# Latent queries of the sample rows, computed in the last head pair of the prompt part instead of at the start of the sample part

## The chip, the cores and the metric

The kernel runs on one core of one Trainium2 chip. The metric is device time of one execution in microseconds (us), and the times are medians of several executions. The trace comes from one profiled execution.

## The reference

One inference step of a decoder trunk with two layers, in float32, for 1024 prompt rows and 8 × 4 = 32 sample rows. Layer 0 has sliding-window attention, layer 1 multi-head latent attention; each is followed by a mixture of 64 experts. The change lies in layer 1. For the sample rows, cut to what matters:

```
q_lat  = einsum('bthd,chd->bthc', qn, w_uk)
s_past = (einsum('bthc,bsc->bhts', q_lat, past_c) + einsum('bthr,bsr->bhts', qr, past_r)) * scale
s_new  = (einsum('bthc,bsc->bhts', q_lat, c) + einsum('bthr,bsr->bhts', qr, kr)) * scale
p      = softmax(concatenate([s_past, s_new]))
o_lat  = p @ [past_c, c];  o = einsum('bthc,chd->bthd', o_lat, w_uv);  y = o @ w_o
```

There are 16 heads of 64 (nope) + 32 (rope) columns, a latent of 256 columns, 8 batch rows with 4 new positions each and 1024 past positions in 8 pages of 128. The prompt rows take the ordinary way: keys `c @ w_uk` and values `c @ w_uv` for each head, causal attention over 1024 positions.

## The kernel before

The kernel is a row of phases. Each phase is a block in which the five engines run their own instruction lists and wait for semaphores; it ends with all engines meeting. Layer 1's attention has three of them: `mla_projection_phase`, `mla_prompt_phase` (tiles with the prefix `h_`) and `mla_sample_phase` (prefix `g_`).

**The prompt part** loops over 8 head pairs `cc` and in each over 16 units `u` (a query block `n` of 128 rows and one head `s` of the pair); `m = 16 * cc + u`. TensorE does, in this order for each m: `scores(m + 2)` (L2340), `turn(m)`, which transposes the probabilities (L2360), in units 8 and 9 the product of the next pair's keys (`keys`, L2317), and a piece of the values product (L2382). VectorE adds the causal mask and takes the maximum (L2285, L2286), ScalarE the exponential (L2201); both copy transposed probabilities out of PSUM. Scores lie in `ps_s[:, m % 2]`, two banks each; keys go to the second bank of one half, `ps_s[:, half, 512:]`, which is free from unit 8 (or 9) until unit 12 (or 13), since the units between are narrow. `keys_out` on ScalarE (even head) and VectorE (odd head) copies them to `kT` right after the step u − 1 = 8 or 9, and `scores` of unit 12 or 13 waits for that. In the last pair there is no next pair: units 8 and 9 have no key product, and the two banks stand empty. SP loads in this phase, among others, the sample rows' queries (`ahead["qn"]`, `ahead["qr"]`), the first pages of the cache, and, after the last keys, w_uk a second time in a turned layout (`uk_in`, L2173).

**The sample part** works on pairs of batch rows, i = 0 to 3. TensorE first waits for `uk_in` and computes the latent queries (L2629): for 8 head pairs, 2 halves `k` of the latent and 2 heads `s`, a product of 64 × 128 weights with 32 columns, into the first two banks of `ps_p`, one bank for each `s`. Each call is two instructions in the trace. Then ScalarE (s = 1) and VectorE (s = 0) copy them to `qlat` (`query_part`, L2503, L2525). TensorE waits for these copies (`ql_done`) and for `qr_done`, that is for `qrb`, in which VectorE lays out the rotary queries (a memset L2518 and four copies L2520). Then come `scores(0, 0)`, `scores(0, 1)` (latent part L2574, rotary part L2580), `new_scores` (L2593), `scores(1, 0)`, `turn(0)` (L2599), `scores(1, 1)`, `values(0)` (L2611) and so on. SP and POOL issue the pages (L2464, 272 KB each): from the start of the phase those of batch rows 2 (second half) to 5, and those of rows 6 and 7 when `values(0)` and `values(1)` are done (`o_made`), on SP with the output weights `w_o` behind them. `scores(i, 0)` waits for all pages of batch rows 2i and 2i + 1.

The functions:

Of the kernel before, what the change touches and what calls it, by code (L numbers as in the profile page):

```python
# [21 lines left out]
P = 128  # L22
D = 1024
SEQ = 1024
NB = 8
NT = 4
NS = NB * NT
# [4 lines left out]
HEADS = 16  # L32
# [8 lines left out]
NOPE = 64  # L41
ROPE = 32
# [2034 lines left out]
def mla_prompt_phase(nc, io, dram, cst, cT, krT, oT_all, w_uv, wk, v, ahead, qT_out, q_stored, places, over_v, pages_in, uk_in):  # L2077
# [38 lines left out]
    with ExitStack() as stack:  # L2116
# [16 lines left out]
        ps_o = c.ps("ps_o", [P, 2, 512])  # L2133
        rot_in, ahead_in = c.sem("rot_in"), c.sem("ahead_in")
        q_in = c.sems("q_in", 2)
        q_done = c.sem("q_done")
# [4 lines left out]
        o_made, o_done = c.sems("o_made", 2), c.sems("o_done", 2)  # L2141
        block = stack.enter_context(nc.Block())

        @block.sync
# [38 lines left out]
        def _(eng):  # L2183
# [39 lines left out]
            for m in range(NU * PAIRS):  # L2223
                cc, u = m // NU, m % NU
                exps(m)
                if m:
                    probs_out(m - 1)
                if u - 1 in KEYS_AT and cc + 1 < PAIRS:
                    keys_out(cc + 1, KEYS_AT.index(u - 1))
                if u == RD_AT[1] + 1:  # L2230
                    recips_out(2 * cc)
                if u == RD_AT[0] + 1 and cc:
                    recips_out(2 * cc - 1)
# [4 lines left out]
        def _(eng):  # L2238
# [41 lines left out]
            for m in range(NU * PAIRS):  # L2280
                cc, u = m // NU, m % NU
                g, n, s = UNITS[u]
                width = P * (n + 1)
                eng.wait_ge(s_made, m + 1)
                ch.link(eng.tensor_tensor(ps_s[:, m % 2, P * n:width], ps_s[:, m % 2, P * n:width], cst["causal"][:], ALU.add))  # L2285
                eng.tensor_reduce(nm[:, u:u + 1], ps_s[:, m % 2, 0:width], AX.X, ALU.max, negate=True).then_inc(nm_done, 1)  # L2286
                if m:
                    probs_out(m - 1)
                if u - 1 in KEYS_AT and cc + 1 < PAIRS:
                    keys_out(cc + 1, KEYS_AT.index(u - 1))  # L2290
                if u % 8 == 3 and m > 3:
                    recips(m // 8 - 1)
                if u in Q_AT and cc + 1 < PAIRS:
                    queries_turned(cc + 1, Q_AT.index(u) // 2, 1 - Q_AT.index(u) % 2)
                if u == NU - 1:
                    rows_out(2 * cc)
                if u == 7 and cc:
                    rows_out(2 * cc - 1)
# [5 lines left out]
        def _(eng):  # L2304
# [9 lines left out]
            def keys(cc, half):  # L2314
# [4 lines left out]
                ins.then_inc(kn_made, 1)  # L2319

            def scores(m):
                cc, u = m // NU, m % NU
# [8 lines left out]
                if u - 4 in KEYS_AT and cc + 1 < PAIRS:  # L2331
                    for sem in (kn_even, kn_odd):
                        eng.wait_ge(sem, 2 * cc + KEYS_AT.index(u - 4) + 3)
                if u == (RD_AT[0] + 4) and cc:
                    eng.wait_ge(rd_done, 2 * cc)
# [57 lines left out]
            for m in range(NU * PAIRS):  # L2393
                cc, u = m // NU, m % NU
                r = m // 8 - 1
                if m + 2 < NU * PAIRS:
                    scores(m + 2)
                turn(m)
                if u in KEYS_AT and cc + 1 < PAIRS:
                    keys(cc + 1, KEYS_AT.index(u))  # L2400
                if u == RD_AT[1]:
                    recips_turn(2 * cc)
                if u == RD_AT[0] and cc:
                    recips_turn(2 * cc - 1)
                if r >= 0 and u % 8 < 6:
                    values(r, u % 8)
# [5 lines left out]
def mla_sample_phase(nc, io, dram, cst, cT, krT, c_sample, oT_all, w_uv, w_ukT, ahead, places, over_v, pages_in, uk_in, w_o):  # L2412
# [7 lines left out]
    with ExitStack() as stack:  # L2420
# [3 lines left out]
        qrb = c.sb("qrb", [P, NB, P // ROPE, R])  # L2424
        qlat = c.sb("qlat", [P, 2, NB, HEADS, NT])
        p = c.sb("p", [P, SEQ + NS])
# [5 lines left out]
        ol = c.sb("ol", [P, KVL])  # L2432
        uk = w_ukT[:].rearrange("p c n -> p (c n)").rearrange("p (h k j) -> p h k j", h=HEADS // 2, k=2)
        olT = w_ukT[:].rearrange("p c n -> p (c n)")[:, 0:2 * HEADS * NS].rearrange("p (k h b t) -> p k h b t", k=2, h=HEADS, b=NB)
# [10 lines left out]
        def half_pages(b, half):  # L2445

            if b == 2 and half:
# [4 lines left out]

        (new_made, qr_done, ql_made, ql_done, s_made, sn_done, p_done, pT_made, pA_done, pD_done, o_made, o_done, oT_made, oT_done, y_made, y_done, chain,
         den_done) = (c.sem(n) for n in (
             "new_made", "qr_done", "ql_made", "ql_done", "s_made", "sn_done", "p_done", "pT_made", "pA_done", "pD_done", "o_made", "o_done", "oT_made",
             "oT_done", "y_made", "y_done", "chain", "den_done"))
# [36 lines left out]

        def query_part(k, s):

            src = ps_p[:, 512 * s + 256 * k:512 * s + 256 * k + 256].rearrange("p (c b t) -> p c b t", c=HEADS // 2, b=NB)
            return qlat[:, k].rearrange("p b (c s) t -> p s c b t", s=2)[:, s], src

        @block.scalar
        def _(eng):  # L2500
            eng.wait_ge(ql_made, 1)
            for s in range(2):
                eng.copy(*query_part(s, 1)).then_inc(ql_done, 1)  # L2503
            for i in range(BP):
# [11 lines left out]
        def _(eng):  # L2516
# [5 lines left out]
            ch.link(eng.memset(oT_all[:, :, SEQ + NS:], 0.0))  # L2522
            eng.wait_ge(ql_made, 1)
            for s in range(2):
                eng.tensor_copy(*query_part(s, 0)).then_inc(ql_done, 1)  # L2525

            eng.wait_ge(new_made, 1)
# [31 lines left out]
        def _(eng):  # L2559
            flat = lambda ap: ap.rearrange("p h t -> p (h t)")  # L2560

            def scores(i, half):
# [8 lines left out]
                for k in range(2):  # L2571
                    for j in range(2):
                        b = 2 * i + j
                        eng.matmul(ps_s[R * j:R * j + R, i % 2, cols], flat(qlat[:, k, b]), half_pages(b, half)[:, :, P * k:P * k + P],  # L2574
                                   start=k == 0, stop=False)
                for r in range(P // ROPE):
                    for j in range(2):
# [44 lines left out]

            eng.wait_ge(uk_in, 16)
            for cc in range(HEADS // 2):
                for k in range(2):
                    for s in range(2):
                        r = slice(NOPE * s, NOPE * s + NOPE)
                        at = 512 * s + 256 * k + NS * cc
                        ins = eng.matmul(ps_p[:, at:at + NS], uk[r, cc, k, :], qn[r, cc, :], start=True, stop=True)  # L2629
            ins.then_inc(ql_made, 1)  # L2630
            eng.wait_ge(qr_done, P // ROPE)
            eng.wait_ge(ql_done, 4)
            scores(0, 0)
# [207 lines left out]
def build(nc, io):  # L2841
# [10 lines left out]
    with ExitStack() as stack:  # L2852
# [10 lines left out]
        for layer in range(2):  # L2863
            with ExitStack() as outer:
# [4 lines left out]
                else:  # L2869
                    with ExitStack() as lat:  # L2870
                        a = lambda n, sh: lat.enter_context(nc.sbuf_tensor(n, sh, F32))
                        cT, krT, c_sample = a("cT", [P, 2, ROWS]), a("krT", [QD, ROWS]), a("c_sample", [NS, KVL])
                        w_uv, w_uk = a("w_uv", [P, 2, HEADS * HD]), a("w_uk", [P, 2, HEADS * NOPE])
                        ahead = {"qn": a("qn", [P, HEADS // 2, NS]), "qr": a("qr", [QD, HEADS, NS]), "mask": a("mask", [P, NB // 2, NS])}
                        ahead["table"] = lat.enter_context(nc.sbuf_tensor("table", [1, NB * PAGES], I32))
# [56 lines left out]
```

## Time and profile before

| | us |
|---|---|
| median of 3 executions | 2445.76 |
| lowest, highest | 2437.91, 2449.31 |
| the profiled execution, its own time | 2443.78 |
| its span in the trace | 2442.1 |
| TensorE matmul busy | 2136.4 |
| VectorE, ScalarE, GpSimd busy | 834.7, 625.5, 222.1 |
| TensorE's mean granted clock (1 is full) | 0.948 |

Times inside the trace are counted from the start of the span. The prompt part of the second attention ends near 1624, and the sample part runs from there to 1699. A timeline row gives start, length, engine, line, operation, tiles and, in brackets, how long the engine was idle before and what ended that. Rows of equal instructions are merged ("x32"). A matmul's length includes its way through the array, so that the pace of a row of them is read from one start to the next.

### The profile page before, as it was taken

The page shows a single profiled execution, that of the slowest core. Times are in us where ns is not written, and L with a number is a line of the kernel's source. Part 1 is how long each engine was busy: PE and PEld are TensorE (multiplying, and loading weights), DVE is VectorE, ACT ScalarE, POOL GpSimd, SP SyncE. Part 2 cuts the span into 40 slices and gives each one's busy share as a digit, 9 for nine tenths or more (in the row PEclk, how much of TensorE's full clock was granted, in tenths as well). Part 3 has the DMA queues.
Part 4 walks back from the last instruction along what each step waited for, and adds up shares of the span by engine and source line. Part 5 has one row for each costly group of instructions (what it writes and reads, how often), then busy time and mean ns, then how long its engine had stood idle before and what let it go on. Part 6 is the DMA issues. An engine that isn't in the chain of part 4 may idle for free. (4 is left out here: it accounts for less than half of the span.)

```text
span 2442.1 us, 27707 instructions
## 1 busy us (share of the span) xinstructions
PE 2136.4 (87%) x9976; PEld 1045.8 (43%) x9976; DVE 834.7 (34%) x2196; ACT 625.5 (26%) x1399; POOL 222.1 (9%) x330
## 2 busy tenths in 40 slices
PE   6999989998887877879998999997998888788886
PEld 3444445563333333345544555554555333333333
DVE  1544445651221111123416666642553221111114
ACT  2444442111111111123425555531111111111114
POOL 0010101101111111100000000010000111101103
PEclk9999988999999999989999999998998999989998
DMA  6000007339999999975550010345527999999997
GB/s 230 18 9 18 5 1 274 120 135 398 419 418 419 419 418 415 408 295 169 135 94 14 14 27 14 100 146 179 207 93 295 418 418 418 419 417 416 416 387 301
DMA packets 175980, 580.97 MB, mean 238 GB/s; under 512 B 80066, under 2 KB 83746, under 8 KB 124914
## 3 DMA queue, kind: packets, MB, share of 16 engines
q1 hardware_dynamic: 90354, 501.76, 51.8%
q10 hardware_dynamic: 64160, 35.42, 4.9%
q0 software_dynamic: 21328, 41.99, 4.6%
q8 instruction: 83, 1.36, 0.2%
q14 instruction: 55, 0.45, 0.1%
HBM read 541.39 MB, written 73.37 MB: 252 GB/s over the span
## 5 line engine op out<-in xcount | busy, mean ns | idle before, releaser
L1586 PE MATMUL m_ps_gu<-ring,m_xT 128*64 128x512 f32 x2080 | 509.9, 647 | 102.3 <-issue 99.0
L1586 PEld LDWEIGHTS m_ps_gu<-ring,m_xT 128*64 128x64 f32 x2080 | 173.2, 148 | 433.3 <-issue 427.8
L1595 PE MATMUL m_ps_y<-ring,m_hT 128*64 128x512 f32 x1040 | 250.7, 626 | 68.5 <-DVE m_hT L1441 68.0
L1485 PE MATMUL m_ps_y<-w_o,oT_all 128*128 128x512 f32 x512 | 231.4, 601 | 3.6 <-PEq L174 3.6
L1435 DVE TENSOR_TENSOR m_h<-m_act,m_ps_gu 128x256 f32<-128x256 f32 x64 | 26.9, 421 | 591.7 <-ACT m_act L1172 591.7
L584 PE MATMUL a_ps_q<-a_w,a_hT 128*128 128x512 f32 x384 | 181.5, 614 | 4.8 <-DMA a_w<-swa_w_qkv 3.5
L2340 PE MATMUL h_ps_s<-h_kT,h_qT 96*128 96x512 f32 (+3 forms) x384 | 158.6, 523 | 14.3 <-ACT h_p L2201 12.2
L1172 ACT ACTIVATE m_act<-m_ps_gu 128x256 f32<-128x256 f32 x64 | 24.5, 383 | 557.0 <-PE m_ps_gu L1586 557.0
L1595 PEld LDWEIGHTS m_ps_y<-ring,m_hT 128*64 128x64 f32 x1040 | 72.3, 142 | 202.1 <-issue 121.2
L1089 POOL DMA_INDIRECT expert_rows<-m_y,m_rows_i x64 | 64.5, 1007 | 869.6 <-DVE m_y L1445 844.7
L1485 PEld LDWEIGHTS m_ps_y<-w_o,oT_all 128*128 128x128 f32 x512 | 95.0, 193 | 107.2 <-issue 107.2
L1445 DVE COPY m_y<-m_ps_y 128x512 f32<-128x512 f32 x64 | 44.3, 692 | 258.5 <-PE m_ps_y L1595 258.5
L2201 ACT ACTIVATE h_p<-h_ps_s,h_nm 128x128 f32<-128x128 f32 (+7 forms) x128 | 94.8, 741 | 106.8 <-DVE h_nm L2286 106.0
L1143 ACT COPY m_y<-m_ps_y 128x512 f32<-128x512 f32 x64 | 37.4, 585 | 280.4 <-PE m_ps_y L1595 280.4
L584 PEld LDWEIGHTS a_ps_q<-a_w,a_hT 128*128 128x128 f32 x384 | 70.2, 194 | 89.2 <-issue 86.9
L2340 PEld LDWEIGHTS h_ps_s<-h_kT,h_qT 96*128 96x128 f32 x384 | 63.1, 190 | 94.7 <-issue 68.9
L2286 DVE TENSOR_REDUCE h_nm<-h_ps_s 128x1 f32<-128x128 f32 (+7 forms) x128 | 97.0, 758 | 4.4
L374 ACT ACTIVATE a_p<-a_s,a_nm 128x256 f32<-128x256 f32 x128 | 64.0, 501 | 115.0 <-DVEq L510 114.2
L1050 POOL DMA_INDIRECT m_xg<-normed,m_toks_i x64 | 65.3, 1020 | 272.1 <-DVEq L1296 242.1
L1571 PEld LDWEIGHTS m_ps_x<-ident,m_xg 128*128 128x128 f32 x512 | 63.3, 195 | 58.7 <-issue 58.7
L2360 PE MATMUL h_ps_p<-ident,h_p 128*128 128x128 f32 x576 | 84.4, 273 | 0.8 <-ACT h_p L2201 0.7
L1571 PE MATMUL m_ps_x<-ident,m_xg 128*128 128x128 f32 x512 | 75.8, 292 | 8.0 <-DMA m_xg<-normed,m_toks_i 8.0
(418 smaller groups left out, 2587.8 us busy)
## 6 DMA issues: line engine op xcount, KB each, us to landing
ring<-moe_w_down SPq DMA_DIRECT2D x130, 1024.0 KB, 23.7
ring<-moe_w_gate SPq DMA_DIRECT2D x124, 1024.0 KB, 21.6
ring<-moe_w_up SPq DMA_DIRECT2D x124, 1024.0 KB, 23.9
ring<-expert_rows SPq DMA_DIRECT2D x16, 1024.0 KB, 8.9
x_ffn<-misc ACTq DMA_DIRECT2D x18, 512.0 KB, 5.4
normed<-m_y ACTq DMA_DIRECT2D x18, 512.0 KB, 3.6
places<-mla_pages SPq DMA_DIRECT2D x30, 272.0 KB, 3.3
a_w<-swa_w_qkv SPq DMA_DIRECT2D x12, 512.0 KB, 11.0
```

The source lines that it names most:

```text
L374: eng.activation(p[:, m % 2, j, :], s[:, m % 2, j, :], ACT.Exp, bias=nm[:, hh:hh + 1], accum_out=den[:, hh:hh + 1]).then_inc(p_done, 1)
L584: ins = eng.matmul(ps_q[:], hT[:, t % 2, k, :], w[:, k, 512 * n:512 * n + 512], start=k == 0, stop=k == KC - 1)
L1050: eng.indirect_dma_start(out=xg[:, k % 3, :], out_offset=None, in_=dram["normed"], in_offset=bass.IndirectOffsetOnAxis(ap=toks_i[:, k:k + ...
L1089: eng.indirect_dma_start(out=dram["expert_rows"], out_offset=bass.IndirectOffsetOnAxis(ap=rows_i[:, k:k + 1], axis=0), in_=y[:, k % 2, :], ...
L1485: ins = eng.matmul(ps_y[:, n, :], oT_all[:, k, P * t:P * t + P], w_o[:, k, 512 * n:512 * n + 512], start=k == 0, stop=k == KC - 1)
L1571: ins = eng.transpose(ps_x[:, P * i:P * i + P], xg[:, k % 3, i::KC], ident[:])
L1586: ins = eng.matmul(gu_now[r], xT_now[:, i, r], w[:, slot, s, 0:2, DE * i:DE * i + DE], start=i == 0, stop=i == KC - 1)
L1595: ins = eng.matmul(ps_y[r, n, :], hT[:, i, r], w[:, slot, s, 2, D * i + 512 * n:D * i + 512 * n + 512], start=i == 0, stop=i == 1)
L2201: eng.activation(p[:, m % 2, 0:width], ps_s[:, m % 2, 0:width], ACT.Exp, bias=nm[:, m % NU:m % NU + 1], accum_out=den[:, g, PLACE[n], s:s ...
L2286: eng.tensor_reduce(nm[:, u:u + 1], ps_s[:, m % 2, 0:width], AX.X, ALU.max, negate=True).then_inc(nm_done, 1)
L2340: ins = eng.matmul(ps_s[:, m % 2, a:b], qT[cc % 2][:, s, P * n:P * n + P], kT[cc % 2][:, s, a:b], start=True, stop=True)
L2360: ins = eng.transpose(ps_p[:, at + P * t:at + P * t + P], p[:, m % 2, P * t:P * t + P], ident[:])
```

## The change

- `query_latents(s)` does the same 32 calls in `mla_prompt_phase`, in the last head pair, those of s = 0 in the step of unit 8 and those of s = 1 in the step of unit 9, after `turn` and before the values product. They write to the second bank of `ps_s[:, s]`, where the other pairs have their keys. All calls of one step have the same `s`.
- ScalarE copies the result for s = 0 and VectorE that for s = 1, at the places where `keys_out` stands in the other pairs. `scores` of units 12 and 13 wait for these copies.
- `qlat` becomes a buffer of the outer scope (4 KB of each partition), so that it outlives the prompt part.
- In the sample part the products, the copies and their wait are gone. The wait for `qr_done` moves from before `scores(0, 0)` to before its rotary part.

```diff
+            def query_latents(s):
+                if s == 0:
+                    eng.wait_ge(ahead_in, 16 * 6)
+                    eng.wait_ge(uk_in, 16)
+                r = slice(NOPE * s, NOPE * s + NOPE)
+                for h in range(PAIRS):
+                    for k in range(2):
+                        at = 512 + 256 * k + NS * h
+                        ins = eng.matmul(ps_s[:, s, at:at + NS], uk[r, h, k, :], ahead["qn"][r, h, :], start=True, stop=True)
+                ins.then_inc(ql_made, 1)
...
# TensorE, scores(m) of the prompt part
+                if u - 4 in KEYS_AT and cc + 1 == PAIRS:
+                    eng.wait_ge((ql_even, ql_odd)[KEYS_AT.index(u - 4)], 2)
...
-                if u in KEYS_AT and cc + 1 < PAIRS:
-                    keys(cc + 1, KEYS_AT.index(u))
+                if u in KEYS_AT:
+                    if cc + 1 < PAIRS:
+                        keys(cc + 1, KEYS_AT.index(u))
+                    else:
+                        query_latents(KEYS_AT.index(u))
...
# ScalarE; VectorE the same with KEYS_AT[1], ql_made 2, tensor_copy, query_part(k, 1) and ql_odd
+                if u - 1 == KEYS_AT[0] and cc + 1 == PAIRS:
+                    eng.wait_ge(ql_made, 1)
+                    for k in range(2):
+                        eng.copy(*query_part(k, 0)).then_inc(ql_even, 1)
...
# the sample part
-            eng.wait_ge(uk_in, 16)
-            for cc in range(HEADS // 2):
-                for k in range(2):
-                    for s in range(2):
-                        r = slice(NOPE * s, NOPE * s + NOPE)
-                        at = 512 * s + 256 * k + NS * cc
-                        ins = eng.matmul(ps_p[:, at:at + NS], uk[r, cc, k, :], qn[r, cc, :], start=True, stop=True)
-            ins.then_inc(ql_made, 1)
-            eng.wait_ge(qr_done, P // ROPE)
-            eng.wait_ge(ql_done, 4)
             scores(0, 0)
...
+                if i == 0 and half == 0:
+                    eng.wait_ge(qr_done, P // ROPE)
                 for r in range(P // ROPE):
```

## Rows read from the trace of the kernel before

**Rows 1.** The page's first line.

```profile
span 2442.1 us, 27707 instructions
```

**Rows 2.** Timeline of TensorE, last pair but one, unit 8.

```profile
1562.00 1.88 PE L2317 MATMUL h_ps_s<-cT,w_uk 128*128 128x512 f32 x4
1563.81 1.08 PE L2382 MATMUL h_ps_o<-h_pT,v_rows 128*64 128x256 f32 x8
```

**Rows 3.** Timeline of TensorE, last pair, unit 8.

```profile
1602.61 0.82 PE L2360 MATMUL h_ps_p<-ident,h_p 128*128 128x128 f32 x6
1603.36 1.08 PE L2382 MATMUL h_ps_o<-h_pT,v_rows 128*64 128x256 f32 x8
```

**Rows 4.** Timeline of VectorE: maxima of units 8 and 15, in the last two pairs.

```profile
1558.56 0.96 DVE L2286 TENSOR_REDUCE h_nm<-h_ps_s 128x1 f32<-128x768 f32 x1
...
1579.12 0.69 DVE L2286 TENSOR_REDUCE h_nm<-h_ps_s 128x1 f32<-128x512 f32 x1
...
1599.82 0.96 DVE L2286 TENSOR_REDUCE h_nm<-h_ps_s 128x1 f32<-128x768 f32 x1
...
1616.35 0.69 DVE L2286 TENSOR_REDUCE h_nm<-h_ps_s 128x1 f32<-128x512 f32 x1
```

**Rows 5.** TensorE's waits, 1581 to 1624: us in total, times, longest.

```profile
PE h_ps_s L2340 <- ACT h_p L2201: 0.9, 2, 0.6
PE h_ps_p L2360 <- ACT h_p L2201: 0.7, 1, 0.7
```

**Rows 6.** Timeline of the engines, start of the sample part.

```profile
1624.96 5.20 PE L2629 MATMUL g_ps_p<-qn,w_uk 64*128 64x32 f32 x64 [1.62 <-PEq L174]
...
1627.22 1.80 DVE L2520 COPY g_qrb<-qr 32x512 f32<-32x512 f32 x4
...
1631.13 1.09 PE L2574 MATMUL g_ps_s<-over_v,g_qlat 128*64 128x512 f32 x1 [0.97 <-issue]
...
1634.22 0.27 PE L2580 MATMUL g_ps_s<-over_v,g_qrb 128*64 128x128 f32 x1
...
1639.99 0.64 PE L2574 MATMUL g_ps_s<-over_v,g_qlat 128*64 128x512 f32 x1
...
1640.11 0.29 DVE L2528 TENSOR_TENSOR g_sn<-g_ps_n,mask 128x128 f32<-128x128 f32 x1 [9.08 <-PE g_ps_n L2593]
...
1643.88 1.09 PE L2599 MATMUL g_ps_p<-ident,g_p 128*128 128x128 f32 x8 [1.08 <-ACT g_p L2510]
```

**Rows 7.** Engines in stretches of 1 us: busy, TensorE's clock, DMA share, GB/s.

```profile
1627.00:1628.00 1.00, 1.00 (x15) 1.00 (x14) 0.93 (x3) 0.00 (x0) 0.81 (x2) 0.51 0.71 126
...
1633.00:1634.00 1.00, 1.00 (x6) 0.35 (x4) 0.00 (x0) 0.00 (x0) 0.00 (x0) 0.57 1.12 350
```

**Rows 8.** Page loads issued from 1631.3 to 1631.9.

```profile
L2464 SPq DMA_DIRECT2D places<-mla_pages x1: 333/333/333, 1631.5 to 1631.5; - x1
...
DMA to landing us min/median/max: 6.3/6.7/7.3
```

**Rows 9.** The same view as rows 7, when the first page loads end.

```profile
1649.00:1650.00 1.00, 1.00 (x12) 0.67 (x10) 0.31 (x2) 0.56 (x1) 0.00 (x0) 1.00 0.29 111
```

**Rows 10.** TensorE's waits after 1640: us in total, times, longest.

```profile
PE g_ps_s L2574 <- DMA places<-mla_pages: 12.3, 1, 12.3
```

**Rows 11.** L2629 alone: TensorE busy, weight loads busy, clock, DMA share, GB/s.

```profile
1624.96:1627.00 2.04, 2.04 (x37) 2.04 (x38) 1.00 0.01 4
```

**Rows 12.** Timeline of TensorE in the expert phase: small matmuls and what follows.

```profile
1732.69 1.90 PE L1510 MATMUL m_ps_gu<-m_wr,m_xT 128*128 128x72 f32 x16
1734.43 5.36 PE L1485 MATMUL m_ps_y<-w_o,oT_all 128*128 128x512 f32 x12
1739.63 0.53 PE L1528 MATMUL m_ps_h<-m_cols,m_slots 128*128 128x32 f32 x4
1739.99 0.41 PE L1517 MATMUL m_ps_gu<-m_ohs,before 128*128 128x64 f32 x2
```

**Rows 13.** SP's load of w_uk in the turned layout.

```profile
L2173 SPq DMA_DIRECT2D w_uk<-mla_w_uk_turned x1: 339/339/339, 1568.1 to 1568.1; - x1
```

More of the change, by code:

```diff
@@ L2134, in mla_prompt_phase @@
         rot_in, ahead_in = c.sem("rot_in"), c.sem("ahead_in")
+        ql_made, ql_even, ql_odd = c.sem("ql_made"), c.sem("ql_even"), c.sem("ql_odd")
+        uk = wk[:].rearrange("p c n -> p (c n)").rearrange("p (h k j) -> p h k j", h=PAIRS, k=2)
         q_in = c.sems("q_in", 2)
@@ L2142, in mla_prompt_phase, with query_part @@
         block = stack.enter_context(nc.Block())
+        def query_part(k, s):
+            src = ps_s[:, s, 512 + 256 * k:512 + 256 * k + 256].rearrange("p (c b t) -> p c b t", c=PAIRS, b=NB)
+            return ahead["qlat"][:, k].rearrange("p b (c s) t -> p s c b t", s=2)[:, s], src
         @block.sync
@@ L2290, in _ @@
                     keys_out(cc + 1, KEYS_AT.index(u - 1))
+                if u - 1 == KEYS_AT[1] and cc + 1 == PAIRS:
+                    eng.wait_ge(ql_made, 2)
+                    for k in range(2):
+                        eng.tensor_copy(*query_part(k, 1)).then_inc(ql_odd, 1)
                 if u % 8 == 3 and m > 3:
@@ L2319, in keys @@
                 ins.then_inc(kn_made, 1)
+            def query_latents(s):
[4 more added lines that the diff above has]
+                for h in range(PAIRS):
+                    for k in range(2):
+                        at = 512 + 256 * k + NS * h
+                        ins = eng.matmul(ps_s[:, s, at:at + NS], uk[r, h, k, :], ahead["qn"][r, h, :], start=True, stop=True)
+                ins.then_inc(ql_made, 1)
             def scores(m):
@@ L2424, in mla_sample_phase @@
         qrb = c.sb("qrb", [P, NB, P // ROPE, R])
-        qlat = c.sb("qlat", [P, 2, NB, HEADS, NT])
+        qlat = ahead["qlat"]
         p = c.sb("p", [P, SEQ + NS])
@@ L2432, in mla_sample_phase @@
         ol = c.sb("ol", [P, KVL])
-        uk = w_ukT[:].rearrange("p c n -> p (c n)").rearrange("p (h k j) -> p h k j", h=HEADS // 2, k=2)
         olT = w_ukT[:].rearrange("p c n -> p (c n)")[:, 0:2 * HEADS * NS].rearrange("p (k h b t) -> p k h b t", k=2, h=HEADS, b=NB)
@@ L2451, in half_pages @@
             return tensor[:, at:at + H]
-        (new_made, qr_done, ql_made, ql_done, s_made, sn_done, p_done, pT_made, pA_done, pD_done, o_made, o_done, oT_made, oT_done, y_made, y_done, chain,
+        (new_made, qr_done, s_made, sn_done, p_done, pT_made, pA_done, pD_done, o_made, o_done, oT_made, oT_done, y_made, y_done, chain,
          den_done) = (c.sem(n) for n in (
-             "new_made", "qr_done", "ql_made", "ql_done", "s_made", "sn_done", "p_done", "pT_made", "pA_done", "pD_done", "o_made", "o_done", "oT_made",
+             "new_made", "qr_done", "s_made", "sn_done", "p_done", "pT_made", "pA_done", "pD_done", "o_made", "o_done", "oT_made",
              "oT_done", "y_made", "y_done", "chain", "den_done"))
@@ L2492, in _ @@
             load_pages(eng, odd, 1, 7)
-        def query_part(k, s):
-            src = ps_p[:, 512 * s + 256 * k:512 * s + 256 * k + 256].rearrange("p (c b t) -> p c b t", c=HEADS // 2, b=NB)
-            return qlat[:, k].rearrange("p b (c s) t -> p s c b t", s=2)[:, s], src
         @block.scalar
         def _(eng):
-            eng.wait_ge(ql_made, 1)
-            for s in range(2):
-                eng.copy(*query_part(s, 1)).then_inc(ql_done, 1)
             for i in range(BP):
@@ L2522, in _ @@
             ch.link(eng.memset(oT_all[:, :, SEQ + NS:], 0.0))
-            eng.wait_ge(ql_made, 1)
-            for s in range(2):
-                eng.tensor_copy(*query_part(s, 0)).then_inc(ql_done, 1)
             eng.wait_ge(new_made, 1)
@@ L2621, in rows_turn @@
                 ins.then_inc(oT_made, 1)
-            eng.wait_ge(uk_in, 16)
-            for cc in range(HEADS // 2):
-                for k in range(2):
-                    for s in range(2):
-                        r = slice(NOPE * s, NOPE * s + NOPE)
-                        at = 512 * s + 256 * k + NS * cc
-                        ins = eng.matmul(ps_p[:, at:at + NS], uk[r, cc, k, :], qn[r, cc, :], start=True, stop=True)
-            ins.then_inc(ql_made, 1)
-            eng.wait_ge(qr_done, P // ROPE)
-            eng.wait_ge(ql_done, 4)
             scores(0, 0)
@@ L2873, in build @@
                         w_uv, w_uk = a("w_uv", [P, 2, HEADS * HD]), a("w_uk", [P, 2, HEADS * NOPE])
-                        ahead = {"qn": a("qn", [P, HEADS // 2, NS]), "qr": a("qr", [QD, HEADS, NS]), "mask": a("mask", [P, NB // 2, NS])}
+                        ahead = {"qn": a("qn", [P, HEADS // 2, NS]), "qr": a("qr", [QD, HEADS, NS]), "mask": a("mask", [P, NB // 2, NS]),
+                                 "qlat": a("qlat", [P, 2, NB, HEADS, NT])}
                         ahead["table"] = lat.enter_context(nc.sbuf_tensor("table", [1, NB * PAGES], I32))
```

## The prediction

> **What bounds the kernel now.** I read the page first. Its chain of what ended last reaches back only through the final phase, so it doesn't speak of this place; the page gives the span, 2442.1 us [rows 1]. The change touches two stretches, the last head pair of the prompt part and the first 20 us of the sample part. So I read the timelines of TensorE, VectorE and ScalarE over both.
>
> In the prompt part TensorE sets the pace. In the pair before the last, the key product of unit 8 starts at 1562.00 and the next thing starts at 1563.81 [rows 2]: a slot of 1.81 us with nothing idle behind it. In the last pair the transposes at 1602.61 run straight into the values product at 1603.36 [rows 3]. That the keys' slots are fully exposed can be read from VectorE's maxima: from unit 8 to unit 15 it takes 1579.12 − 1558.56 = 20.56 us with keys and 1616.35 − 1599.82 = 16.53 us without [rows 4]. The difference, 4.03 us, is two slots (3.62 us) and 0.4 more. From 1581 on TensorE waits 1.6 us in all in the last pair [rows 5].
>
> In the sample part the order is different. TensorE begins at 1624.96 with the latent queries, starts the first scores of pages at 1631.13, their rotary part at 1634.22, the second batch pair's scores at 1639.99, and turns the first probabilities at 1643.88, after a wait of 1.08 us for ScalarE; VectorE had started on the new rows' scores at 1640.11 [rows 6]. The granted clock of TensorE is at the lower level (0.5, 1.2 GHz) from 1627.0 on and comes back to 2.4 GHz late in the stretch that starts at 1633 [rows 7].
>
> **What is taken out of the sample part.** The 32 calls (64 instructions) of the latent queries, four copies, and the wait for them. TensorE can start the page scores at once, at 1624.96 if the start of the phase is held still. After some 1.7 us it meets the new wait: the rotary part needs qrb, whose four copies start at 1627.22 and take 1.80 us [rows 6], so until 1629.0. Behind this wait in TensorE's queue are the rest of scores(0, ·) and new_scores. From the rotary part (1634.22) to the end of new_scores (1639.99) it took 5.8 us, nearly all at the full clock. So new_scores would end near 1629.1 + 5.8 = 1634.9, or about 1637.4 if the lower clock holds for 5 of these us (half of 5 is lost): 2.6 to 5.1 us earlier than before.
>
> What is late next is a transfer. scores(1, 0) waits for the pages of batch rows 2 and 3. SP and POOL issue them from the start of the phase on, at times that the change doesn't touch. The last of these on SP goes out at 1631.5, and the three issued between 1631.3 and 1631.9 take 6.3 to 7.3 us to land [rows 8]: the last is there near 1631.5 + 7.3 = 1638.8. In the kernel before that was hidden, as TensorE came at 1639.99, only 1.2 us later. In the changed kernel TensorE comes early and waits until 1638.8. Then 1642.80 − 1639.99 = 2.81 us of scores (the end is 1643.88 less the idle 1.08 [rows 6]) end at 1641.6, and turn(0) follows at once: its exponentials are through 3.9 us after new_scores (1643.88 less 1639.99), which is 1638.8 to 1641.3. So turn(0) starts at 1641.6 instead of 1643.88, and the gain is **2.3 us**, not the 6.2 us between 1624.96 and 1631.13 that the removed work took. From below: were the landing no gate, turn(0) would come at 1638.8 to 1641.3, a gain of 5.1 to 2.6. From above: a clock that falls in the new waits takes 1.5 us or more of it back.
>
> Does the rest follow? values(0) and o_made come 2.3 us earlier. That releases the next pages, and the output weights behind them on SP. The first batches of pages keep the DMA engines busy only until about 1649.3, as the share of 0.29 in the stretch from 1649 shows [rows 9]; so the next loads can start earlier. The 12.3 us that TensorE later waits for pages [rows 10] is the tail of that transfer, and it moves with its start. Everything behind (projection, experts, final norm) begins at the end of this phase. I let the 2.3 us through whole.
>
> **What is put into the last pair.** The same 64 instructions, in two slots of 32, after turn(8) and turn(9), where TensorE is the bound [rows 2 to 5]. Their price is what has to be chosen. Before, s alternated from call to call: s = 0 reads partitions 0 to 63 and s = 1 reads 64 to 127. 37 of them fell into 2.04 us at the full clock, 0.055 us each [rows 11]. In the new loops all calls of a slot have the same s, so neighbours use the same half of the array. The nearest rows of matmuls that can't share the array are the slot sums' (L1528, 128 loaded columns, 32 moving): 4 of them take 1739.99 − 1739.63 = 0.36 us, 0.09 each; and the router's (L1510, 128 loaded, 72 moving): 16 take 1734.43 − 1732.69 = 1.74 us, 0.109 each [rows 12]. I take 0.09, as both sizes match: 64 × 0.09 = **5.8 us**. The bounds are 64 × 0.055 = 3.5 and 64 × 0.109 = 7.0.
>
> The Trainium skill (TensorE: Matmul & The Clock Gate, Part 3, The mechanism) says that a weight load overlaps matmuls in flight only when it goes to another row group. That speaks against the grouping by s, and it is on the side of the 5.8. If loads overlapped whatever the group, as the page's queue with its background buffer might let one hope, the slots would cost 3.5.
>
> The copies: ScalarE gets two of 256 columns behind slot 0 and VectorE two behind slot 1. Behind the wait for ql_made on ScalarE stands exps(10), behind the one on VectorE the maximum of unit 11. In the pair before, keys_out stands at these places; scores(13) needs the exponentials of unit 11, and TensorE gets to scores(13) 3.6 us after its slot (a values product, scores(12), turn(10) and values again), while 0.8 us of copies, 0.9 us of maxima and 0.8 us of exponentials make 2.5. I cost them at nothing; if the cover were gone it would be the 0.8 us of VectorE's copies. The two other new waits on TensorE are long over: w_uk's second content is issued at 1568.1 [rows 13], 35 us before the slot. The 4 KB that qlat now takes in the outer buffers moves addresses only.
>
> **Sum.** +5.8 in the prompt part, −2.3 in the sample part: +3.5 us. The profiled execution is 2443.8 us by its own time (span 2442.1 and 1.7 around it), so 2447.3. It lies 2.0 below the median shown, 2445.8, so a median of **2449 us**, 0.14% above before. The three times shown spread over 11 us; 0.5% (12 us) is about what a measurement of this kernel can tell from no change, so this is no change by that measure.
>
> **The rivals.**
>
> (a) Shared slots: the grouping costs nothing (3.5 us), and the pages are no gate (a gain near 5): −1.5 us, 2444. For it: the gate stands only 1.2 us before the old start. Against it: the pages' issue times don't hang on TensorE, and the order by s is plain in the code.
>
> (b) The clock falls in the sample part. There are now two waits of TensorE, one of 2.4 us (1626.7 to 1629.1) and one of up to 3.9 us (1634.9 to 1638.8). In the kernel before it fell at 1627.0, after an idle 1.6 us and 2 us of these small matmuls, and was low until 1633.6 [rows 6, 7]. If scores(1, 0), turn(0) and the next run at half for 3.4 us, 1.7 is lost; for 6.8 us, 3.4, which is the whole gain. Then +5.2 to +6.9: 2451 to 2453. The Trainium skill (the same page, Part 1, What's actually happening) says that the array's default is the throttled state and that activity releases it; the fall at 1627.0 agrees.
>
> (c) The slower side: the clock falls in the last pair. The slots are 2.9 us each of small matmuls in a stretch where TensorE is the bound. If each pulled the clock down for the 6.8 us seen in [rows 7], that would cost 3.4 us a slot, 6.8 in all: 2456, and with (b) 2459, beyond the 12 us. Its decisive point is whether such a slot counts as activity. Against it: the router's 16 matmuls [rows 12] run in 1.74 us among big ones, and the pace behind them stays full.
>
> (d) The change as a whole hides: both slots fill idle time. The 1.6 us of waits [rows 5] are not after the slots, except 0.7 at the pair's end, which depends on TensorE's own scores. I leave it under (a).
>
> **Chances.** Forecast, with terms between their nearest bounds, 0.58; (a) and the like 0.15; (b) 0.17; (c) 0.10, of which half stays within 12 us. The terms alone give +3.5 − 5.1 = −1.6 us at the low end and, with 7.0 for the slots and a gain of 2.3 − 3.4 = −1.1, +8.1 at the high end, so 2444 to 2454; two medians of three executions differ by some 3 us without a cause. Range 2440 to 2457. Slower by over 0.5%: 0.06; faster by over 0.5%: 0.04, which no mechanism here gives, only scatter; within: 0.90.
>
> **What the profile will show.** Right: L2340/L2360 of the last pair at the old pace; two slots of 32 small matmuls, 2.9 us each; the span of maxima from unit 8 to 15 near 22.3 us instead of 16.53; page scores at the phase's first instruction; a wait for qrb of some 2.4 us; a wait for pages before the ninth page-score group; turn(0) 16.6 us after TensorE's first instruction of the phase instead of 18.9. Wrong: slots of 1.8 us (the halves overlap anyway), no wait for pages, or a granted clock of 0.5 in the last pair.

## The result, and the profile after

The changed kernel takes 2457.29 us in the median (2450.44 to 2465.46, 13 executions), the kernel before 2445.33 (2437.17 to 2449.31, 13 executions): a ratio of 1.0053, 95% interval 1.0043 to 1.0062. That is 12 us slower, at the very bound that I had called no change, and just outside my range.

The profiled execution of the changed kernel is a quick one (2450.44 us, span 2448.8). The place of the change has to be compared by itself, and this is its timeline on TensorE, from turn(8) of the last pair on. The later rows answer to [rows 3] and [rows 6].

```profile
1600.97 0.82 PE L2389 MATMUL h_ps_p<-ident,h_p 128*128 128x128 f32 x6
1601.72 5.00 PE L2345 MATMUL h_ps_s<-qn,w_uk 64*128 64x32 f32 x32
1606.65 1.97 PE L2411 MATMUL h_ps_o<-h_pT,v_rows 128*64 128x256 f32 x8
1608.56 1.65 PE L2369 MATMUL h_ps_s<-h_kT,h_qT 96*128 96x384 f32 x2
1610.00 1.22 PE L2389 MATMUL h_ps_p<-ident,h_p 128*128 128x128 f32 x6
1611.15 4.26 PE L2345 MATMUL h_ps_s<-qn,w_uk 64*128 64x32 f32 x32
1615.34 1.55 PE L2411 MATMUL h_ps_o<-h_pT,v_rows 128*64 128x256 f32 x8
...
1637.14 0.61 PE L2593 MATMUL g_ps_s<-over_v,qlat 128*64 128x512 f32 x1 [1.64 <-PEq L174]
...
1641.24 0.32 PE L2601 MATMUL g_ps_s<-over_v,g_qrb 128*64 128x128 f32 x1 [2.17 <-DVE g_qrb L2543]
...
1651.28 0.61 PE L2593 MATMUL g_ps_s<-over_v,qlat 128*64 128x512 f32 x1 [2.47 <-DMA places<-mla_pages]
...
1655.71 1.09 PE L2620 MATMUL g_ps_p<-ident,g_p 128*128 128x128 f32 x8
...
1686.52 3.30 PE L2593 MATMUL g_ps_s<-places,qlat 128*64 128x512 f32 x8 [11.98 <-DMA places<-mla_pages]
...
1711.49 1.96 PE L1485 MATMUL m_ps_y<-w_o,oT_all 128*128 128x512 f32 x4 [1.72 <-PEq L174]
```

The two slots take 4.93 us (1601.72 to 1606.65) and 4.19 us (1611.15 to 1615.34), 9.1 in all. And the values product behind the first, which takes 1.08 us in [rows 3], takes 1.97: not only the small matmuls are slow, but everything around them. From turn(8) to TensorE's first instruction of the sample part it is 36.17 us; before it was 1624.96 − 1602.61 = 22.35. The last pair costs **13.8 us** more.

The same view as [rows 7], for single microseconds of the last pair: the seventh number is TensorE's granted clock.

```profile
1602.00:1603.00 1.00, 1.00 (x12) 1.00 (x11) 0.97 (x3) 0.26 (x1) 0.00 (x0) 1.00 0.69 237
1604.00:1605.00 1.00, 1.00 (x7) 1.00 (x7) 0.00 (x0) 0.00 (x0) 0.00 (x0) 0.50 0.00 0
...
1612.00:1613.00 1.00, 1.00 (x12) 1.00 (x10) 0.00 (x0) 0.00 (x0) 0.00 (x0) 1.00 0.00 0
1615.00:1616.00 1.00, 1.00 (x6) 0.75 (x8) 0.55 (x2) 0.00 (x0) 0.00 (x0) 0.50 0.00 0
1620.00:1621.00 1.00, 1.00 (x6) 0.62 (x8) 0.52 (x1) 0.93 (x2) 0.00 (x0) 0.50 0.00 0
1652.00:1653.00 1.00, 1.00 (x4) 0.30 (x2) 0.28 (x2) 0.66 (x4) 0.89 (x3) 0.50 1.05 409
```

The clock falls to its lower level within each slot and stays there for work behind it. In the sample part it is low again while scores(1, 0) runs (the last row).

The sample part, from TensorE's first instruction to the first of the expert phase, takes 1711.49 − 1637.14 = 74.35 us; before it took 75.23, as the expert phase began at 1700.19. So it gives 0.9 us back. 13.8 − 0.9 = 12.9 us agrees with the 12 of the medians, but the 0.9 is one trace's figure and doesn't repeat: in the profiled executions of the nine other kernels that have the latent queries in the last pair, the same stretch takes 74.4 to 79.6 us, and in seven of them more than the 75.23 before. The span of the profiled execution is only 6.7 us longer, because it reached turn(8) 1.6 us earlier and spent 4.6 us less behind 1711, in phases that the change doesn't touch.

### The profile page after: what moved, and what is told of

Same layout as the page of the kernel before. It is cut to its first block and busy times, and to the rows that moved or that the text cites. A ratio compares the mean times of both kernels' runs of the same rounds, so it can differ in the third digit from the quotient of the medians.

```text
span 2448.8 us, 27709 instructions
## 1 busy us (share of the span) xinstructions
PE 2137.2 (87%) x9976; PEld 1044.4 (43%) x9976; DVE 836.9 (34%) x2196; ACT 624.9 (26%) x1399; POOL 222.2 (9%) x330
```

## The experiments

Each kernel was timed in five rounds beside the kernel before; e4_one_grouped has six executions and e2_spread seven, the others eleven or twelve. A ratio of 1.001 is 2.4 us. The pitch is the time from the start of one small matmul instruction to the start of the next. "Slow part" is the last pair, from turn(8) to the sample part, in the profiled execution: 22.35 us before, 36.17 in the changed kernel.

**e1_one_slot.** As in the kernel before, each s keeps a bank of its own. So s = 0 and s = 1 can only alternate when both second banks of `ps_s` are free, and that is between turn(9) and scores(12). So all 32 calls go there.

```diff
+                for h in range(PAIRS):
+                    for k in range(2):
+                        for s in range(2):
+                            r = slice(NOPE * s, NOPE * s + NOPE)
...
+                if u == KEYS_AT[1] and cc + 1 == PAIRS:
+                    query_latents()
```

> All 32 calls of the latent queries stand in one slot behind turn(9), in the order of the kernel before (head, k, s, so that the two halves of the array alternate and write to two banks). Theory 1 (the grouping by s doubles the pitch of the small matmuls from 0.055 to 0.11 us, and the long slots pull the clock down): the slot is 3.5 us at the full clock, the sample part gives 0.9 to 2.3 us back, so 1 to 3 us above the kernel before, and up to 3.4 more where the clock falls once. Rival (what costs is that small matmuls of 64 rows stand in this place at all, in any order): about as the changed kernel, 12 us above the kernel before.

**e4_one_grouped.** The same slot, with the loop over s outermost.

```diff
-                for h in range(PAIRS):
-                    for k in range(2):
-                        for s in range(2):
+                for s in range(2):
+                    for h in range(PAIRS):
+                        for k in range(2):
```

> As the one slot behind turn(9), but all calls of s = 0 first and then all of s = 1; nothing else differs. Theory 1: 64 instructions at 0.11 us are 7 us at the full clock, and with a fall of the clock inside 9 to 14 us, so 8 to 13 us above the kernel before and 6 to 10 above the alternating slot. Rival (order doesn't matter): the same as the alternating slot, within 1 us.

Timeline of TensorE, e1_one_slot:

```profile
1609.55 3.76 PE L2345 MATMUL h_ps_s<-qn,w_uk 64*128 64x32 f32 x64
1613.24 1.55 PE L2411 MATMUL h_ps_o<-h_pT,v_rows 128*64 128x256 f32 x8
```

and e4_one_grouped:

```profile
1605.14 10.24 PE L2345 MATMUL h_ps_s<-qn,w_uk 64*128 64x32 f32 x64
1615.31 1.55 PE L2411 MATMUL h_ps_o<-h_pT,v_rows 128*64 128x256 f32 x8
```

The same 64 instructions in the same place take 3.69 us in one order and 10.17 in the other. The ratios are 1.0021 (1.0007 to 1.0036) and 1.0053 (1.0033 to 1.0074). The order of s carries more than half of the loss. The alternating kernel is above what theory 1 gave it, at 5 us instead of 1 to 3 (up to 6 with a fall of the clock, and it had one). Its instructions alternate in pairs, since each call is two instructions.

**e2_spread.** Grouped by s, in eight pieces of eight instructions around the big matmuls of units 8 to 10.

```diff
+                if last and u == 8:
+                    query_latents(0, 0)
...
+                if last and u == 9:
+                    query_latents(0, 3)
+                    query_latents(1, 0)
```

> Grouped by s as in the changed kernel, with the same 64 instructions, but in eight pieces of 8 instructions over units 8 to 10, between the big matmuls. The pitch stays 0.11 us, so 7 us are added. If the fall of the clock comes from the length of the slots (theory 1), it stays at the full level here, and the kernel is 5 to 6 us above the kernel before, 6 below the changed one. If the clock falls by the small matmuls' share whatever their order, or falls for another reason, it is as the changed kernel, 12 above.

The ratio is 1.0045 (1.0026 to 1.0065), the slow part 38.03 us with the mean clock at 0.78 (row below). My idea that the clock falls because a slot is long is wrong: short pieces pull it down too.

**e3_one_pair.** `for h in range(PAIRS)` becomes `for h in range(1)` in `query_latents`.

> The changed kernel with the products of the first head pair alone (8 of 64 instructions, 0.9 us in all); those of the other seven head pairs are left out, and their queries are whatever the banks held. It shows what the sample part gives back without the price of the slots. By the prediction: 2.3 less 0.9, so 1.4 us faster than the kernel before. By the profile of the changed kernel, where the sample part was only 0.9 us shorter: the same as before, within 1 us. A rival by which the slots are not the cost: still 5 us or more above the kernel before.

The ratio is 1.0008 (0.9996 to 1.0021), the slow part 23.50 us. Without the products the loss is gone but for 2 us, of which 1.1 are in the last pair. The sample part alone brings no measurable gain.

**e5_wide.** Twice the moving columns.

```diff
+                        n = 2 if h + 1 < PAIRS else 1
+                        ins = eng.matmul(ps_s[:, s, at:at + NS * n], uk[r, h, k, :], ahead["qn"][r, h:h + n, :].rearrange("p h n -> p (h n)"), start=True, stop=True)
```

> The changed kernel, each small matmul with 64 moving columns instead of 32 (the next head's 32 too, which the next head's product overwrites; the last head keeps 32). If the pitch of 0.11 us is that of two weight loads that can't overlap, it stays 0.11 at the full clock. If it is the moving columns, it grows by 0.027 us or more each, 1.7 us in all. The clock: if it falls because the small matmuls stream few columns, with twice as many it falls less, and the last pair is up to 6.8 us shorter than the 36.2 us from turn(8) to the sample part, the kernel 5 to 6 above the kernel before. If it falls as before, it is 12 to 14 above.

The small matmuls alone, at the full clock (busy, instructions, weight loads, clock, DMA), in the first 2.3 us of the first slot of e5_wide:

```profile
1607.90:1610.20 2.30, 2.30 (x21) 2.30 (x21) 1.00 0.42 121
```

and in the first 2.35 us of the second slot of the changed kernel:

```profile
1611.15:1613.50 2.35, 2.35 (x21) 2.35 (x22) 1.00 0.00 0
```

0.11 us each with 64 columns as with 32: moving columns don't set the pitch. The clock fell as before, slow part 37.79 us, ratio 1.0044 (1.0030 to 1.0059).

**e6_before_grouped.** The kernel before, with its loop over s outermost at its old place, in the sample part.

> The kernel before, its latent queries where they were, at the start of the sample part, but all calls of s = 0 first, then all of s = 1. By the theory that the grouping doubles the pitch (0.11 us at the full clock, 0.2 at half): the 64 instructions take 9 to 11 us instead of 5.2, the scores come 4 to 6 us later, past the pages' landing, and the kernel is 3 to 6 us slower than the kernel before. By the rival that order doesn't matter: no change.

```profile
1627.29 11.63 PE L2629 MATMUL g_ps_p<-qn,w_uk 64*128 64x32 f32 x64 [1.62 <-PEq L174]
```

11.63 us instead of 5.20 [rows 6], ratio 1.0024 (1.0013 to 1.0035), 6 us slower. The order alone costs this much in a kernel in which nothing was moved.

**e7_one_slot_fill.** e1_one_slot with fillers in the sample part's two new waits.

```diff
+            def fill(n):
+                for _ in range(n):
+                    eng.matmul(ps_p[:, 0:512], ident[:], cT[:, 0, 0:512], start=True, stop=True)
...
+                    fill(2)
                     eng.wait_ge(qr_done, P // ROPE)
```

> The kernel with one alternating slot, and in the sample part five matmuls of 512 columns on other data whose result is not used: two before the wait for qrb, three before the wait for the pages of scores(1, 0). They are 0.86 us each and fit into these waits. If the clock that falls in the new waits takes the sample part's saving, it now stays full: turn(0) stands 16.6 to 17 us after TensorE's first instruction of the phase, the sample part is 2 us shorter than in the other kernels, and the kernel 4 us above the kernel before instead of 6. If the clock is not what takes it, nothing changes, or it is slower by what the fillers overrun.

Timeline of TensorE, e7_one_slot_fill, with turn(0) in the last row:

```profile
1628.25 0.61 PE L2597 MATMUL g_ps_s<-over_v,qlat 128*64 128x512 f32 x1 [1.64 <-PEq L174]
...
1642.06 0.61 PE L2597 MATMUL g_ps_s<-over_v,qlat 128*64 128x512 f32 x1 [1.05 <-DMA places<-mla_pages]
...
1644.80 1.09 PE L2625 MATMUL g_ps_p<-ident,g_p 128*128 128x128 f32 x8
```

turn(0) stands 16.55 us after the first instruction, as forecast for a full clock, against 18.57 in the changed kernel and 18.92 before. Of the 2.02 us between 18.57 and 16.55, 0.33 come from the pages, which are there 13.81 us after the first instruction instead of 14.14, and 1.69 from scores(1, 0) itself. So the lower clock does take most of the saving up to turn(0). But the wait for pages ahead of scores(3, 0) ends 49.0 us after the first instruction (1677.20), against 50.1 before (1675.02): half of the 2.4 us won at turn(0) is gone by then. The ratio is 1.0018 (1.0006 to 1.0030) against 1.0021, which can't be told apart.

**e8_before_fill.** Twelve fillers ahead of scores(3, 0), in the kernel before.

> The kernel before with twelve such fillers (10.3 us) ahead of scores(3, 0), where TensorE waits 12.3 us for pages and the granted clock is at half for 3.1 us after the wait. If that half clock lies on the path, the stretch from the end of the wait to the end of the phase is 1.5 us shorter, and the kernel 1.5 us faster, near the edge of what the rounds can tell. If not, no change. If the fillers' reads or an overrun delay the pages, slower.

Ratio 0.9994 (0.9984 to 1.0004): inconclusive. The fillers ended 2 us before the pages were there, and in the profiled execution scores(3, 0) still ran at the lower clock (eight of its matmuls in 3.33 us instead of 1.94).

**e9_full_rows.** `r = slice(0, P)` in `query_latents`.

> The changed kernel, each small matmul over all 128 partitions instead of 64, so that its result mixes the two heads of a pair (it leaves the separation of the heads out). Count, columns and order are the same. If the pitch is that of loads which can't overlap on the same rows, it stays 0.11 us at the full clock. The clock fell in the last pair of every kernel with the grouped order (13.7 to 17.1 us at half) and for 3.4 us only with the alternating one. If it falls because only one half of the array's rows works at a time, it now falls less, and the last pair takes 30 to 33 us from turn(8) on; if it falls because small matmuls leave gaps, whatever their rows, it takes 36 to 38 again.

The slots take 3.59 and 3.74 us, 0.11 for each of 32; the clock fell once, near the end of the second slot, 9.4 us after the first of these instructions; slow part 32.54 us; ratio 1.0033 (1.0019 to 1.0046), 8 us slower instead of 12.

**e11_half_load.** The output becomes `ps_s[0:64, ...]` and the weights `uk[r, h, k, 0:64]`.

> The changed kernel with 64 weight columns in each small matmul instead of 128: the second half of each block of 128 latent columns is left out, and the copies take what the bank held. If the weight load sets the pitch of the grouped order, it halves, to about 0.055 us at the full clock, and the two slots take 3.5 us in all plus what the clock adds: 3 to 8 us above the kernel before instead of 12. If the pitch is the sequencer's or the matmul's own, it stays at 0.11.

The slots take 1.98 us each, 0.062 for an instruction, the clock never falls, slow part 26.34 us, ratio 1.0007 (0.9997 to 1.0018). The median is 1.7 us above the kernel before, less than the 3 to 8 expected. The weight load sets the pitch.

**e12_column_halves.** All the work, grouped by s, each call split by weight columns.

```diff
+                        for j in range(2):
+                            half = slice(64 * j, 64 * j + 64)
+                            ins = eng.matmul(ps_s[half, s, at:at + NS], uk[r, h, k, half], ahead["qn"][r, h, :], start=True, stop=True)
```

> The changed kernel, complete, in its two slots and grouped by s, but each call split into two with 64 weight columns each (output partitions 0 to 63 and 64 to 127), so that neighbours lie on different columns of the array: 128 instructions instead of 64. If loads on the same part of the array are what makes the grouped order dear, loads of neighbours now overlap, the pitch is 0.03 us and the two slots take 4 us in all instead of 9.1; if the clock fell because little of the array worked, it falls less. Then 22.4 + 4 = 26.4 us from turn(8) to the sample part, and 3 to 6 us above the kernel before instead of 12. If instead each instruction has a price of its own (0.06 us as with half the load, or more), the slots take 8 us and the kernel is 7 to 12 above.

```profile
1602.71 2.06 PE L2347 MATMUL h_ps_s<-qn,w_uk 64*64 64x32 f32 x64
1604.70 1.08 PE L2413 MATMUL h_ps_o<-h_pT,v_rows 128*64 128x256 f32 x8
...
1607.21 2.05 PE L2347 MATMUL h_ps_s<-qn,w_uk 64*64 64x32 f32 x64
1609.19 0.87 PE L2413 MATMUL h_ps_o<-h_pT,v_rows 128*64 128x256 f32 x8
```

Twice the instructions in less than half the time: 3.97 us for both slots, 0.031 each, the values product behind at its old 1.08 us, slow part 26.34 us. The ratio is 1.0019 (1.0008 to 1.0030), 4.6 us above the kernel before and some 8 below the change as it stands.

**e10_before_late.** What the waits for pages suggest for the kernel before: at i = 2 turn(2) and values(2) come first, then scores(3, 0) and scores(3, 1).

> The kernel before with another order of TensorE's work at i = 2 of the sample part: turn(2) and values(2), which don't need the last pages, stand before scores(3, 0) and scores(3, 1) instead of between them. The 12.3 us wait for pages then has 5 us of work in it, and the maxima and exponentials of i = 3 (2.9 us) lose their cover. From the end of the wait to the expert phase 25.2 us become 20 to 22, so 3 to 5 us faster than the kernel before, where the changed kernel was 12 slower. If the wait simply ends later for it, or the lower clock eats it, no change.

TensorE's longest waits, e10_before_late, sample part (us in total, times, longest):

```profile
PE g_ps_n L2620 <- DVE g_ol L2550: 3.4, 3, 2.2
PE g_ps_s L2574 <- DMA places<-mla_pages: 3.0, 1, 3.0
```

Ratio 0.9985 (0.9976 to 0.9994), 3.7 us faster: the one version here that beats both kernels. The 12.3 us wait of [rows 10] is 3.0. Its profiled execution doesn't show the gain in the sample part (26.1 us behind the wait, at a mean clock of 0.72, where the kernel before took 25.2 at 0.94), so what the medians gain there rests on the timing alone.

**The account of the slow part.** One row for each kernel, from turn(8) to the sample part: length, busy times, and as seventh number the mean granted clock. In order: before, changed, e1_one_slot, e4_one_grouped, e2_spread, e5_wide, e9_full_rows, e11_half_load, e12_column_halves.

```profile
1602.61:1624.96 22.35, 19.86 (x123) 11.02 (x122) 9.61 (x23) 10.85 (x24) 0.00 (x0) 1.00 0.07 22
```

```profile
1600.97:1637.14 36.17, 33.66 (x188) 22.31 (x186) 10.36 (x25) 11.41 (x26) 0.00 (x0) 0.81 0.05 14
```

```profile
1606.29:1633.98 27.69, 25.18 (x187) 15.35 (x186) 10.37 (x25) 11.51 (x26) 0.00 (x0) 0.94 0.06 19
```

```profile
1601.88:1637.51 35.63, 33.12 (x188) 22.50 (x186) 10.38 (x25) 11.52 (x26) 0.00 (x0) 0.81 0.05 15
```

```profile
1600.02:1638.05 38.03, 35.52 (x188) 23.52 (x186) 10.28 (x25) 11.40 (x26) 0.00 (x0) 0.78 0.04 13
```

```profile
1607.15:1644.94 37.79, 35.28 (x188) 24.20 (x186) 10.37 (x25) 11.43 (x26) 0.00 (x0) 0.77 0.05 14
```

```profile
1597.31:1629.85 32.54, 30.03 (x187) 19.71 (x186) 10.37 (x25) 11.40 (x26) 0.00 (x0) 0.90 0.05 15
```

```profile
1602.51:1628.85 26.34, 23.83 (x188) 14.91 (x186) 10.33 (x25) 11.42 (x26) 0.00 (x0) 1.00 0.06 19
```

```profile
1601.96:1628.30 26.34, 23.83 (x251) 14.91 (x250) 10.31 (x25) 11.41 (x26) 0.00 (x0) 1.00 0.06 20
```

Two terms explain all of them: the instructions at their full-clock pitch, and the length times what the mean clock lacks of 1 (a stretch that TensorE bounds, run at half the clock, loses half of itself: the values product behind the first slot took 1.97 us instead of 1.08). The second term uses the measured length and clock, so that the table splits the times into parts and doesn't forecast them.

| kernel | 22.35 + instructions | + clock loss | sum | measured |
|---|---|---|---|---|
| changed | 64 × 0.111 = 7.1 | 0.19 × 36.17 = 6.9 | 36.4 | 36.17 |
| e1_one_slot | 64 × 0.055 = 3.5 | 0.06 × 27.69 = 1.7 | 27.6 | 27.69 |
| e4_one_grouped | 7.1 | 0.19 × 35.63 = 6.8 | 36.3 | 35.63 |
| e2_spread | 7.1 | 0.22 × 38.03 = 8.4 | 37.9 | 38.03 |
| e5_wide | 7.1 | 0.23 × 37.79 = 8.7 | 38.2 | 37.79 |
| e9_full_rows | 7.1 | 0.10 × 32.54 = 3.3 | 32.8 | 32.54 |
| e11_half_load | 64 × 0.062 = 4.0 | 0 | 26.4 | 26.34 |
| e12_column_halves | 128 × 0.031 = 4.0 | 0 | 26.4 | 26.34 |

## Why the prediction was wrong

**The last pair as the exposed place: right.** The slots have nothing behind which to hide, the sums above leave under 1 us for everything else, and the waits for `uk_in`, `ahead_in` and the copies never appear. The pieces for ScalarE and VectorE cost nothing, as forecast.

**The price of an instruction: the right mechanism, mis-sized.** I took 0.09 us from L1528 [rows 12] and forecast 5.8 us, with 7.0 as the upper bound from L1510; it is 0.111, so 7.1. I had matched the moving columns, and these don't matter (e5_wide); the load of 128 weight columns sets the pitch (e11_half_load), and L1528's four instructions in 0.36 us were misread. TensorE's queue of weight loads, in the kernel before, shows why:

```profile
1739.20 0.19 PEld L1528 LDWEIGHTS m_ps_h<-m_cols,m_slots 128*128 128x128 f32 x1 [0.24 <-issue]
1739.63 0.41 PEld L1528 LDWEIGHTS m_ps_h<-m_cols,m_slots 128*128 128x128 f32 x3 [0.24 <-issue]
1739.96 0.30 PEld L1517 LDWEIGHTS m_ps_gu<-m_ohs,before 128*128 128x128 f32 x2
```

The first load was over before the first of the four matmuls started, so the 0.36 us hold three loads; these take 0.11 us each (1739.63 to 1739.96, where the next loads start). That neighbours on the same part of the array take twice as long as neighbours on different parts is shown three times: by the order alone (e1 against e4), at the old place (e6), and by splitting the columns (e12 against e11). The Trainium skill's rule that I had weighed (TensorE: Matmul & The Clock Gate, Part 3, The mechanism) is that a weight load overlaps matmuls in flight only where the row group differs. For rows the traces agree with it (e1 against e4). Its "only" doesn't fit e12, where neighbours use the same 64 rows and different columns and come every 0.031 us, against 0.062 in e11.

**The clock in the last pair: the step that failed.** The sum had it at nothing. It was rival (c), with a chance of 0.10, and it is what happened: 6.9 us. I held against it that the router's matmuls run at the full clock. They are 16 between big ones, and load 128 rows and 128 columns. The nearer row was in [rows 7] itself, where the clock fell 2 us into exactly these small matmuls; I put that fall down to the idle time ahead of them as well and counted it, outside (c), for the sample part alone. The changed kernel speaks against the idle time: its sample part begins behind the same idle 1.6 us, with page scores in place of the small matmuls, and the clock stays full there until 1641.7.

```profile
1638.00:1639.00 1.00, 1.00 (x6) 0.17 (x2) 1.00 (x1) 0.00 (x0) 0.10 (x1) 1.00 0.02 8
```

With a slot price of 7.1 and the 6.8 us that (c) named, the sum is +13.9, and 13.8 was measured. That the size fits so well is partly luck: with the same 64 instructions grouped by s, the clock took 6.8 us in e4, 8.4 in e2 and 8.7 in e5.

**The sample part: half right.** The gate is where I put it: the pages of scores(1, 0) are there 14.14 us after the first instruction, forecast 13.84 (1638.8 − 1624.96), and qrb's wait is 2.17, forecast 2.4. But turn(0) came at 18.57 us instead of the forecast 16.6, since scores(1, 0) ran at the lower clock (rival (b); e7_one_slot_fill gives 16.55 when it doesn't). And "I let the 2.3 us through whole" was wrong even then: in e7 1.1 us are left at the end of the long wait for pages. There TensorE waits 1.55 us for the pages of scores(2, 0) as well, a second landing that I hadn't priced; whether it is what takes the other half was not separated. In the medians the sample part brings nothing: e3_one_pair is 2 us above the kernel before, with an interval from −1 to +5. A term that I had fixed turns out to move: the pages of scores(1, 0) land 13.8 to 17.0 us after TensorE's first instruction in the ten kernels with the queries in the last pair, although their issues on POOL stand at the same distance from it. TensorE came for them after 15.03 us in the kernel before. In e12, e5 and e1 they land later than that (15.20, 15.48 and 16.99), and an early TensorE can't gain at this gate. The row of e1_one_slot, whose phase starts at 1633.98:

```profile
1650.97 1.11 PE L2592 MATMUL g_ps_s<-over_v,qlat 128*64 128x512 f32 x1 [6.99 <-DMA places<-mla_pages]
```

From issue to landing, the pages issued in the first 11 us take up to 10.0 us in e1 and up to 7.3 in the kernel before. What makes the landing move was not looked into.

**What stays open** is which property of the small matmuls lowers the clock. It isn't the length of a slot (e2), nor the moving columns (e5). It falls for 64 rows in grouped order most, for all 128 rows less (e9), for alternating halves once and briefly (e1), and not at all with 64 × 64 tiles, whose slots are over in half the time (e11, e12). These are single profiled executions, and where a fall begins differs from one to the next. A slot in which s alternates within each of the two old places wasn't tried: only one of the two banks is free in the first of them, and each s kept a bank of its own in all kernels here.

## What to carry to other kernels

Work that stands in the open looks worth moving, but what counts is what would end last without it: here 6.2 us of products and copies covered page loads to within 0.9 us (15.03 against 14.14 us from the first instruction; 1.2 was forecast), and their new place, though its banks were empty, was on the engine that bounds it. When a move also changes the order of small matmuls, price the order: neighbours on different rows or different columns of the array ran at about half the pitch here, and where the free banks don't allow the one alternation, the other may still be had: e12 alternates columns within the changed kernel's own slots and banks. In a stretch that TensorE bounds, a few microseconds of small matmuls can cost twice their own length through the clock.

## What the runs showed of the hardware

- A float32 matmul instruction with 64 × 128 weights and 32 moving columns takes 0.111 us when its neighbours use the same rows and columns, 0.055 to 0.058 when row halves alternate from call to call (two instructions each); with 64 moving columns still 0.11. With 64 × 64 weights it is 0.062 on the same tile and 0.031 when column halves alternate.
- The granted clock fell in every kernel that had 64 instructions at 0.11 us in the last pair, though TensorE was never idle there: 2.3 to 5.6 us after the first of them in the changed kernel, e5, e4 and e2, and 9.4 us after it in e9, which loads all 128 rows. In the kernels with 0.062 and 0.031 it didn't fall in the last pair at all.
- Loads of pages that are issued at the same distance from the start of the phase can land up to 3 us apart (13.81 us in e7_one_slot_fill, 16.99 in e1_one_slot).
- The time of the sample part in the profiled executions scatters with the clock: from the end of the long wait for pages to the expert phase it was 25.2 us before, 25.0 in the changed kernel (mean clock 0.94 in both) and 27.8 in e7_one_slot_fill (0.81), for the same work.
